# The order of many-token and few-token work inside an expert chunk of a two-block network

## The reference

```python
def moe_ffn(x, router, w_gu, w_down):
    ...
    logits = (xt @ router).astype(jnp.float32)
    top_v, top_i = lax.top_k(logits, TOP_K)
    w = jax.nn.softmax(top_v, axis=-1)
    ...
    for e in range(N_EXPERTS):
        y = y + combine[:, e:e + 1] * swiglu(xt, w_gu[e], w_down[e])
```

## Time and profile before

| | |
|---|---|
| median of 3 runs | 2093.42 us (2089.79 to 2094.72) |
| profiled execution, own time | 2096.46 us |
| its span | 2094.4 us |
| expert part, first unit issued to the end | 1188 to 2094 us |
| TensorE busy | 1996.8 us, 95% |
| VectorE busy | 1203.7 us, 57% |
| ScalarE busy | 969.9 us, 46% |
| HBM traffic | 522.5 MB, 249 GB/s over the span |

### The profile page before, as it was taken

How to read it: one execution, slowest core, us unless ns; L and a number is a source line. 1 busy time by engine, 2 the same in 40 slices (tenths; PEclk the granted TensorE clock), 3 DMA queues, 4 the chain that set the end, 5 groups by cost and what they waited for, 6 DMA issues and landing times.

```text
span 2094.4 us, 27829 instructions
## 1 busy us (share of the span) xinstructions
PE 1996.8 (95%) x10836; PEld 1481.1 (71%) x10836; DVE 1203.7 (57%) x1356; ACT 969.9 (46%) x1140; POOL 20.9 (1%) x33
## 2 busy tenths in 40 slices
PE   8889999988999999999998899999999999999997
PEld 7767998776799878887776566766666566656653
DVE  4875545597554564457666755454554555445454
ACT  5554444555444444444454444443444444444444
POOL 0000000000000000000000000000000000000000
PEclk9999999998999999999879999999999999999999
DMA  7413555441465535553300299999999999999995
GB/s 286 144 48 116 201 188 194 142 145 47 153 217 188 196 130 184 199 181 139 108 22 1 113 370 409 417 418 409 387 411 411 393 382 412 412 395 376 422 420 230
DMA packets 74665, 524.40 MB, mean 250 GB/s; under 512 B 8768, under 2 KB 9216, under 8 KB 12192
## 3 DMA queue, kind: packets, MB, share of 16 engines
q1 hardware_dynamic: 71712, 511.64, 62.5%
q0 software_dynamic: 2816, 10.93, 1.5%
HBM read 521.48 MB, written 1.05 MB: 249 GB/s over the span
## 4 chain that ended last, share of the span: by engine, by line
PE 82%; DVE 10%; ACT 5%; issue 3%; DMA 1%; SPq 0%; DVEq 0%; ACTq 0%
PE psum L556 57%; PE psum L2822 10%; PE psum L2873 5%; DVE AR L1733 2%; PE psum L932 1%; PE psum L995 1%; PE psum L2940 1%; ACT HI L539 1%; DVE LO L2771 1%; PE psum L756 1%; PE psum L2125 1%; PE psum L2834 1%; PE psum L737 1%; ACT HI L2764 1%; PE psum L2962 1%
## 5 line engine op out<-in xcount | busy, mean ns | idle before, releaser
L556 PE MATMUL psum<-HI,XT 128*128 128x512 f32 (+1 forms) x2080 | 533.3, 399 | 25.3 <-ACT HI L2764 6.4
L547 DVE TENSOR_TENSOR LO<-ring,HI 128x2048 fp32r<-128x2048 f32 (+1 forms) x157 | 346.8, 2214 | 280.8 <-ACT HI L539 280.8
L556 PEld LDWEIGHTS psum<-HI,XT 128*128 128x128 f32 x2080 | 391.1, 194 | 148.8 <-issue 37.9
L539 ACT ACTIVATE HI<-ring 128x2048 fp32r<-128x2048 f32 (+1 forms) x157 | 289.7, 1849 | 230.5 <-PE psum L556 229.7
L556 PE MATMUL psum<-LO,XT 128*128 128x512 f32 (+1 forms) x1040 | 281.8, 394 | 1.5 <-DVE LO L2771 1.1
L2771 DVE TENSOR_TENSOR LO<-ring,HI 128x2048 fp32r<-128x2048 f32 x84 | 191.1, 2288 | 86.5 <-ACT HI L2764 80.9
L556 PEld LDWEIGHTS psum<-LO,XT 128*128 128x128 f32 x1040 | 198.4, 193 | 45.5 <-DVE LO L2771 4.7
L556 PE MATMUL psum<-HI,HTH 128*128 128x512 f32 x568 | 228.2, 402 | 0.0
L556 PE MATMUL psum<-HI,HTL 128*128 128x512 f32 x568 | 222.3, 391 | 0.0
L2764 ACT ACTIVATE HI<-ring 128x2048 fp32r<-128x2048 f32 x84 | 159.4, 1910 | 84.9 <-DMA ring<-in_experts 73.7
L2771 DVE TENSOR_TENSOR LO<-AR,HI 128x2048 fp32r<-128x2048 f32 x64 | 145.8, 2288 | 67.7 <-ACT HI L2764 67.5
(11 more groups left out here) (329 smaller groups left out, 2177.4 us busy)
## 6 DMA issues: line engine op xcount, KB each, us to landing
ring<-in_experts SPq DMA_DIRECT2D x172, 1024.0 KB, 9.2
ring<-in_dense SPq DMA_DIRECT2D x149, 1024.0 KB, 4.9
AR<-in_experts SPq DMA_DIRECT2D x84, 1024.0 KB, 9.7
cons<-in_experts SPq DMA_DIRECT2D x42, 1024.0 KB, 9.2
bcs<-in_experts SPq DMA_DIRECT2D x38, 1024.0 KB, 8.5
bcs<-in_ln_g POOLq DMA_DIRECT2D x4, 512.0 KB, 6.4
bcs<-in_ln_b POOLq DMA_DIRECT2D x4, 512.0 KB, 5.4
bcs<-in_norm_g POOLq DMA_DIRECT2D x3, 512.0 KB, 3.9
```

The lines of the kernel that those rows point to most:

```text
L539: e.activation(HI[:, h:h + m], slot(u), ACT.Copy).then_inc(*high.up(u))
L547: e.tensor_tensor(LO[:, h:h + m], slot(u), HI[:, h:h + m].bitcast(F32), ALU.subtract).then_inc(*(freed if u in early else low).up(u))
L556: ins = e.matmul(out_ap, lhsT=a, rhs=b, start=start and n == 0, stop=stop and n == len(pairs) - 1)
```

## The change

In chunks 1 to 6 the order inside each half becomes: the units of the few expert (w=1) first, those of the great expert second. `stage_units` and `stage_cols` are changed alike; in stage 0 the few group w=0, which shares the great units, stays behind them. In chunk 0 the order stays. ScalarE's, VectorE's and SyncE's programs keep their order of steps; which bank a step finds its data in follows from the order of `banks.take`.

```diff
@@ stage_units
         elif c < 7:
-            units += [(w, p, c, i) for i in range(2) for w in range(2) for p in ("up", "gate")]
+            units += [(w, p, c, i) for i in range(2) for w in (1, 0) for p in ("up", "gate")]
@@ stage_cols
             for i in range(2):
+                if c:
+                    few_cols(e, s, 1, c, i)
                 for part in ("up", "gate"):
                     great_cols(e, s, part, c, i)
                 if (s, c, i) == (0, 0, 0):
                     fetch_few_tensor(e)
                 if FEW[s][0]:
                     few_cols(e, s, 0, c, i)
-                if c:
-                    few_cols(e, s, 1, c, i)
```

## The result

The changed kernel takes 2107.62 us (median of 5 runs, 2101.09 to 2115.96) against 2093.42 (5 runs, with the same median as the 3 of the table), a ratio of 1.0067 with a 95% interval of 1.0048 to 1.0087: 14.2 us slower. I forecast 2099.9, 6.5 us slower, with 2097 to 2104 as the forecast's own range and 2089 to 2106 with the rivals. The direction was right. The size was less than half of the measured one, which lies outside both ranges.

What follows compares the result with a forecast made beforehand. TensorE was taken as the bound. Terms 5.4 + 2.6 + 0.5 + 0.9 - 1.7 - 1.9 + 0.7 = +6.5 us, applied to the median 2093.42, gave 2099.9 us; range 2097 to 2104, with rivals 2089 to 2106.

Steps and rivals of the forecast that it cites:

- What bounds: Expert part: TensorE sets the pace, not the DMA queue; only in stage 3 is the queue the slower one.
- Stage 0, the start of chunk 1: First few block waits 3.4 us for a bank ScalarE empties after a late unit's HI; through chunk 2, +2.6 us.
- The clock: Stage 0, after the 3.4 us stall: clock falls, 1.7 us lost, mostly covered by ScalarE's later release; +0.5 us counted.
- The bank waits: TensorE waits for ScalarE's few copies: stage 0, chunks 2 to 6, +5.4 us; chunk 1 of stages 1 to 3, +0.9.
- What goes: Chunk 2 of stages 1 to 3: few work first hides a late HI, 0.8 us in stage 1, half later; -1.7.
- Block costs: Chunk borders of stages 1 to 3: few down block followed by few block saves 0.16 us, 12 times; -1.9 us.
- Stage 3: Stage's end, chunk 6: third great unit loses lead where the queue is slower, stall of 0 to 1.4 us; +0.7.
- (1): Rival: ScalarE's copies finish in time, no bank waits, only chunk 2's stalls go; -7.5 us, 2086; chance 0.11.
- (3): Rival: waits are traded even, stage 0 loses half the forecast, wins stay; -1 to +4 us, 2095; chance 0.25.
- (2): Rival: the clock falls after each stall of stage 0, not only long ones; 8.5 us more, 2108; chance 0.07.
- (4): Rival: stage 3's queue starves for few units' slots, two landings late; +5 us on the sum, 2105; chance 0.07.
- Data: Great units lose 1.4 us of lead, slots free 1 to 2 us sooner; no data late in stages 0 to 2.

Runs made afterwards that it cites:

- `weights_first`: Changed kernel with VectorE's stage 0 weights moved ahead of the LO of chunk 1's first great unit: 2100.95 us, ratio 1.004 to the kernel before.
- `copy_first`: Changed kernel with ScalarE's few copy (w=1) ahead of the Silu, both copies ahead of HI in stage 0 chunk 0: 2098.3 us, ratio 1.0022.
- `best_all`: Kernel before plus new order in stages 1 to 3, few copy before Silu, LO before gate product there, stage 0's residue moved to chunk 3: 2087.01 us.

## Why the prediction was wrong in size

Of the 7.7 us between the forecast 6.5 and the measured 14.2, the stages hold 5.0 (11.5 for 6.5), all of it in stage 0 (13.5 for 8.5). The other 2.7 did not come back when the changed kernel was timed again.

**What bounds.** Right: no wait of TensorE for a DMA shows, and the cost came from waits on ScalarE and VectorE.

**Stage 0, the start of chunk 1: the step that failed.** I wrote "Stage 0, chunk 1, start: its first few block wants the bank that ScalarE empties only after the HI" and priced a stall of 3.4 us there. The landing was right: forecast at 1224.5, it came at 1226.98 in a profile whose stages begin 2.5 later. But I had followed the late unit through ScalarE's program and stopped. VectorE's program has the same unit's LO ahead of the weights, and TensorE wants these before it reaches chunk 1. This wait ends last: 7.83 us. The runs show both: moving the weights away uncovers the bank wait at 3.0.

**What that step cost.** Up to the end of chunk 2, without that chunk's bank wait, the forecast was 3.1 (2.6 and 0.5). Measured are 8.5: TensorE reaches the chunk's turn 11.9 us later than before, less 2.5 of later start and 0.9 of bank wait. With the weights moved (`weights_first`) the same reckoning gives 2.5: the turn comes at 1269.21 for 1266.49, in a profile whose stages begin 0.8 earlier, less 0.95 of bank wait. So the wait for the weights, with its share of the low clock, is the whole of this miss, and the rest of the forecast for these two chunks holds within 0.6 us.

**The clock.** I took a fall of 1.7 us, mostly covered by ScalarE's later release, and counted 0.5. With the stop of 3.0 that is what the trace shows: the few half-pair behind it takes 3.52 for about 1.8, at a granted clock of 0.52, and at the end of chunk 1 TensorE waits only 1.02 where I had worked out 2.9 (1245.7 to 1248.6). Behind the stop of 7.8 the fall costs 3.1 (1.45 for 0.60, 3.57 for 1.8, 6.32 for 5.80), which I had not counted since I had not seen the stop. There too the wait at the end of chunk 1 is 0.94 and not 2.9, since TensorE reaches it later. Of the two stalls "over 2 us" around chunk 1 that I named as a sign, the first stood hidden behind the wait for the weights, and the second was short.

**The bank waits.** Right: 5.4 forecast for chunks 2 to 6 (1.08 each), about 5 measured (0.94 each, and 1.0 a chunk by the chunks' distance); 0.3 forecast in chunk 1 of the later stages, 0.26 measured. That they were causes is shown by `copy_first`.

**What goes.** The 0.8 us in stage 1's chunk 2 went, as did the halves in the others.

**Block costs.** The direction was right and the size too small: a chunk with a fetch loses 0.37 us, for which I had 0.16 from one few block behind another. The fetch block is shorter behind a great pair too (1.30 for 1.50 in the chain), an item that no row of before showed. No run took the order of the blocks apart from the rest, so this cause is read from the chain.

**Stage 3.** Missed: I had "What is late next is nothing until the bank wait at E". The LO of the first down unit, written behind the later gate product, is: a chunk takes 29.53 us from turn to turn, 0.26 longer than before, and 28.97 where `best_all` has this LO ahead of the gate product. The stall of 0.7 at the stage's end did not come: the pair of chunk 6 takes 5.97 for the 5.91 of before.

The sum over stages 1 to 3, forecast -2.0 (0.9 - 1.7 - 1.9 + 0.7), measured -2.0, is right by luck, by errors that cancel: a cheaper block order and a stall that did not come, against a new wait.

**The rivals.** (1) and (3), that the bank waits don't bite or are half repaid, are out. (2) named 2108, next to the measured 2107.62, but by luck: its mechanism, a fall of the clock after each stall, is out. After stalls of 0.94 us the clock stays up. In the stretch directly behind such a stall the profile after has the clock at 1.00:

```profile
1278.43:1290.58 12.15, 12.15 (x128) 8.09 (x128) 6.45 (x7) 6.79 (x6) 0.00 (x0) 1.00 1.01 413
```

The Trainium skill, "TensorE: Matmul & The Clock Gate", section "A second HAM failure mode: psum-queue depth-cycling", says of another kernel that frequent short idles while it cycles PSUM banks make the clock swing. These six stops of 0.94 us, one in 20 to 30 us, don't bear it out; only the long one made it fall. (4), starved slots in stage 3, is out: TensorE shows no wait for a few unit there, and the stage grows by 1.2 us and not by 5.

**Data.** "In stages 0 to 2 no data come late" was wrong in one place: the unit that lands at 1226.98 stands at the head of the whole chain of waits. My own step on chunk 1 had this landing, so the sentence and the step did not agree. For the rest TensorE waits for no landing. Whether the earlier release of the few units' slots feeds the queue sooner by itself was not tried.

## What to carry to other kernels

When units change places in a stream that several engines follow in program order, follow the moved unit through every engine's program, and list at each what stands behind it though it doesn't need it: the weights here kept TensorE waiting 7.8 us for a landing that they had no use for. When a wait is worked out, ask of the same moment which other wait could end later; taking one away may only show the next. And in banks that are handed out by turn, a new order of takes changes who inherits whose bank, though no instruction changes: give the eviction that has become urgent the earlier place.

## What the runs showed that I had not expected

The expert part is repeatable to a tenth of a microsecond a stage (229.14 and 229.12, 219.07 and 219.09 in two profiles of different calls), while the part ahead of it began the stages between 1200.53 and 1207.93 us in programs that are equal up to there but for entries of the plan array. A difference of 2 us in this kernel is read from the stages of one profile and not from the medians.
